# Feed-forward weight sums: two of four made by accumulating transfers instead of VectorE

## The chip, the cores and the metric

The kernel runs on one core of a Trainium2 chip. The metric is the device time of one launch, in microseconds (us). Names of engines: PE is TensorE (PEld its weight loads), DVE is VectorE, ACT is ScalarE, POOL is GpSimd, SP is SyncE; SPq, ACTq and POOLq are the DMA issues of those engines.

## The reference

A block with attention and a mixture of experts is followed by two transformer layers. The change touches the feed-forward part of these two layers alone (256 tokens, width 1024, hidden width 4096, all float32):

```python
for layer in range(DEPTH_2):
    ...
    x = x + mixed @ w_out[layer]
    h = rms_norm_2(x, mlp_norm_w[layer])
    x = x + jnp.square(jax.nn.relu(h @ w_up[layer])) @ w_down[layer]
return rms_norm_2(x, final_norm_w)
```

## The kernel before

**Stages.** First come the conditioning and attention of the first block, then 32 experts (bound by their weight transfers), then the two layers. Every weight is streamed once from HBM, in tiles of 128 x 2048 float32 (1 MB). A layer has 48 tiles: 0 to 11 are input projections, 12 to 15 the output projection `w_out` (its second half is line L1159), 16 and 17 the first four chunks of the up projection by plain matmuls (L629), 18 to 46 the 29 tiles "seven" (14 of the up projection, 15 of the down projection), 47 the last two chunks of the down projection.

**A seven tile.** It is a matrix product of 2 x 2 blocks with seven block products instead of eight (Strassen's scheme in Winograd's form). Four of the products need sums of weight blocks, s1 to s4, and sums of token blocks, t1 to t4. PE's order in `pe_seven` is: `a11` by b11 (no sum), s2, s1, s3, s4, `a12`, `a22`; one product is 8 matmul records (L1223), a tile is 56. The token sums are made once for each set of tokens by `dve_differences` (`diff_ready`).

**Weight sums.** `dve_weight_sums` makes all four on DVE, each by one TENSOR_TENSOR of 128 x 512: s1 = a21 + a22 (L2387), s3 = a11 - a21 (L2389), s2 = s1 - a11 (L2391), s4 = a12 - s2 (L2393); then `sum_ready` goes up. They lie in two buffers used in turn, which PE hands back with `sum_used` after its fifth product. The sums of tile i + 2 stand in DVE's program behind the combination of tile i's products (`dve_seven`, L2416 to L2422). The sums of the layer's tile 0 stand ahead of the norm of the feed-forward input: DVE adds the residual (L2315) and the squares (L2230), makes the sums, then runs the norm (L1772, L1775, L2187) and `dve_differences` (L2400 to L2407), for which PE's first seven tile waits.

**Transfers.** SP issues every weight tile in order. A layer's tiles go round `RL` = 8 ring buffers, so tile t is issued when tile t - 8 is handed back (`slot_free`). A tile is handed back within the first matmuls of the next tile.

**POOL** runs a few transfers for the first block, a fold of 256 columns in each layer (`pool_fold`), and nothing in the feed-forward part.

Of the kernel before, what the change touches and what calls it, by code (L numbers as in the profile page):

```python
# [141 lines left out]
RL = 8  # L142
# [195 lines left out]
def memory(g):  # L338
# [107 lines left out]
    g.sums = [g.ring[RL + n] for n in range(2)]  # L446
    g.cq_turned, g.ck_turned = (g.ring[RL][:, n * 4 * S:(n + 1) * 4 * S].rearrange("p (c t) -> p c t", c=4) for n in range(2))
# [3 lines left out]
    rest = [apart(a, n) for a in (g.ring[RL + 2], g.ring[RL + 3], g.m_all[:, KC * S:2 * KC * S]) for n in range(4)]  # L451
# [89 lines left out]
def sp_program(sp, g):  # L541
# [194 lines left out]
def pe_unread(e, g, n):  # L736

    e.wait_ge(g.s["ones_set"], 1)
    twice = g.c("ones").unsqueeze(1).to_broadcast([P, 2, P])
# [154 lines left out]
def pe_route(e, g):  # L894
    for k in (4, 5, 6):
        pe_logits(e, g, k)
    pe_turn_tokens(e, g, 2, 0)
    pe_logits(e, g, 7)
    u = g.take(e, ("ss", 1), 6)
    e.wait_ge(g.s["sq_added"], ADDED[1])  # L900
    for tt in range(ST):
        ins = e.matmul(u.ap[:, tt:tt + 1], g.sq[:, 0, tt * P:(tt + 1) * P], g.c("ones", 0, 1), start=tt == 0, stop=True, skip_group_check=True)
    g.last(u, ins)
    pe_turn_tokens(e, g, 0, 7)
    pe_turn_tokens(e, g, 1, 1)
# [8 lines left out]
    e.wait_ge(g.s["none_set"], 1)  # L914
# [288 lines left out]
def pe_seven(e, g, l, i):  # L1203
# [5 lines left out]
    (a11, a12), (a21, a22) = quarters(w)  # L1209
    s1, s2, s3, s4 = (g.sums[i % 2][:, n * 512:(n + 1) * 512].rearrange("p (k c) -> p k c", k=4) for n in range(4))  # L1210
# [221 lines left out]
def act_first(e, g, A):  # L1432
# [21 lines left out]
    e.dma_start(g.posi[:, :], g.dram["pos"].to_broadcast([P, S])).then_inc(s["pos_in"], 16)  # L1454
# [107 lines left out]
def act_layer(e, g, l):  # L1562
# [383 lines left out]
def dve_angles(e, g):  # L1946
# [14 lines left out]
    e.wait_ge(s["pos_in"], 16)  # L1961
    e.wait_ge(s["cst_in"], 16)
# [274 lines left out]
def dve_layer(e, g, l):  # L2237
# [100 lines left out]
    for i in range(SEVENS):  # L2338
# [3 lines left out]
        elif b == of - 1:  # L2342
# [3 lines left out]
            two = g.x[:, 2 * mp:2 * mp + 2, :].rearrange("p c t -> p (c t)")  # L2346
            ins = e.tensor_tensor(two, two, g.pair_c, ALU.add)
# [32 lines left out]
def dve_weight_sums(e, g, l, i):  # L2380

    w = g.filled(e, layer_tile(l, 18 + i))
    (a11, a12), (a21, a22) = quarters(w)
    s1, s2, s3, s4 = (g.sums[i % 2][:, n * 512:(n + 1) * 512].rearrange("p (k c) -> p k c", k=4) for n in range(4))
    if i >= 2 or l:
        e.wait_ge(g.s["sum_used"], SEVENS * l + i - 1)
    g.step.up(e.tensor_tensor(s1, a21, a22, ALU.add))  # L2387
    first = g.step.n
    g.step.up(e.tensor_tensor(s3, a11, a21, ALU.subtract))  # L2389
    e.wait_ge(g.step.sem, first)  # L2390
    g.step.up(e.tensor_tensor(s2, s1, a11, ALU.subtract))  # L2391
    g.after(e)
    e.tensor_tensor(s4, a12, s2, ALU.subtract).then_inc(g.s["sum_ready"], 1)  # L2393


def dve_differences(e, g, a, diff, t1=None):
# [6 lines left out]
    g.step.up(e.tensor_tensor(t1, b12, b11, ALU.subtract))  # L2403
# [169 lines left out]
def pool_program(e, g):  # L2573
    s = g.s
    e.memset(g.c("ones"), 1.0).then_inc(s["ones_set"], 1)
# [11 lines left out]
    e.memset(g.none, 0.0).then_inc(s["none_set"], 1)  # L2587
# [115 lines left out]
```

## Time and profile before

| | us |
|---|---|
| median of the runs shown (2) | 1376.43 |
| lowest, highest | 1376.09, 1376.78 |
| span of the profiled execution | 1375.2 |
| PE busy in it | 1336.9 |
| DVE busy in it | 634.6 |
| ACT busy in it | 299.1 |
| POOL busy in it | 7.8 |

The profile's page states the span, from the first to the last instruction; it gives no other time for that execution. The median of the runs is 1.2 us above the span. Busy times can overlap; a time counts for the end only where nothing else covers it.

### The profile page before, as it was taken

The page shows a single profiled execution, that of the slowest core. Times are in us where ns is not written, and L with a number is a line of the kernel's source. Part 1 is how long each engine was busy: PE and PEld are TensorE (multiplying, and loading weights), DVE is VectorE, ACT ScalarE, POOL GpSimd, SP SyncE. Part 2 cuts the span into 40 slices and gives each one's busy share as a digit, 9 for nine tenths or more (in the row PEclk, how much of TensorE's full clock was granted, in tenths as well). Part 3 has the DMA queues.
Part 4 walks back from the last instruction along what each step waited for, and adds up shares of the span by engine and source line. Part 5 has one row for each costly group of instructions (what it writes and reads, how often), then busy time and mean ns, then how long its engine had stood idle before and what let it go on. Part 6 is the DMA issues. An engine that isn't in the chain of part 4 may idle for free.

```text
span 1375.2 us, 21077 instructions
## 1 busy us (share of the span) xinstructions
PE 1336.9 (97%) x8758; PEld 997.9 (73%) x8758; DVE 634.6 (46%) x1424; ACT 299.1 (22%) x596; POOL 7.8 (1%) x18
## 2 busy tenths in 40 slices
PE   8999999999999998888999999999999999999997
PEld 5888886444334433333588789999998878999996
DVE  2477565111100100010378847774555784777454
ACT  2234102112112112111243521220013352122000
POOL 0000000000000000000000000000000000000000
PEclk9999999999999999999999999999999999999999
DMA  9997785999999999999954144545444414454410
GB/s 393 361 413 263 300 358 186 421 414 421 421 421 421 420 421 421 421 421 420 417 224 154 62 153 154 183 156 183 155 159 151 151 62 154 158 180 158 180 62 32
DMA packets 52096, 364.63 MB, mean 265 GB/s; under 512 B 6160, under 2 KB 6464, under 8 KB 8992
## 3 DMA queue, kind: packets, MB, share of 16 engines
q1 hardware_dynamic: 49392, 355.49, 65.6%
q10 hardware_dynamic: 1888, 5.04, 1.3%
q0 software_dynamic: 720, 2.72, 0.5%
q8 instruction: 72, 1.18, 0.4%
q14 instruction: 24, 0.20, 0.1%
HBM read 359.02 MB, written 2.11 MB: 263 GB/s over the span
## 4 chain that ended last, share of the span: by engine, by line
PE 87%; DMA 11%; DVE 1%; ACT 0%; issue 0%; DVEq 0%; POOL 0%; POOLq 0%
PE bank L1223 26%; PE bank L629 20%; PE bank L944 17%; DMA ring<-in_weights 6%; PE bank L641 5%; DMA ringx<-in_weights 4%; PE bank L955 3%; PE bank L1368 2%; PE bank L1159 2%; PE bank L757 2%; PE bank L929 1%; PE bank L1272 1%; PE bank L1323 1%; PE bank L741 1%; PE bank L701 1%; PE bank L1349 1%
## 5 line engine op out<-in xcount | busy, mean ns | idle before, releaser
L944 PE MATMUL bank<-ring,cst 128*64 128x512 f32 x648 | 196.4, 595 | 7.6 <-DMA ring<-in_weights 6.1
L629 PE MATMUL bank<-h,ring 128*128 128x256 f32 x832 | 184.1, 381 | 0.1
L629 PEld LDWEIGHTS bank<-h,ring 128*128 128x128 f32 x832 | 156.9, 190 | 22.8 <-issue 1.7
L944 PEld LDWEIGHTS bank<-ring,cst 128*64 128x64 f32 x648 | 60.7, 137 | 102.0 <-issue 99.7
L2151 DVE TENSOR_TENSOR act<-act,bank 128x512 f32<-128x512 f32 (+1 forms) x17 | 11.1, 656 | 245.0 <-PE bank L944 245.0
L1223 PE MATMUL bank<-hid,ring 128*128 128x128 f32 x912 | 115.6, 275 | 0.0
L1223 PE MATMUL bank<-h,ring 128*128 128x128 f32 x896 | 113.8, 275 | 0.0
L1223 PEld LDWEIGHTS bank<-hid,ring 128*128 128x128 f32 x912 | 108.6, 192 | 0.0
L944 PE MATMUL bank<-ringx,cst 128*64 128x512 f32 x264 | 101.0, 596 | 6.8 <-DMA ring<-in_weights 4.2
L1223 PEld LDWEIGHTS bank<-h,ring 128*128 128x128 f32 x896 | 107.0, 192 | 0.1
L1223 PE MATMUL bank<-sq,ring 128*128 128x128 f32 x720 | 95.1, 275 | 0.0
L944 PE MATMUL bank<-ring,a_s 128*64 128x512 f32 x312 | 90.5, 597 | 0.8 <-DMA ring<-in_weights 0.7
L1223 PEld LDWEIGHTS bank<-sq,ring 128*128 128x128 f32 x720 | 87.6, 192 | 0.0
L641 PE MATMUL bank<-ring,h 128*128 128x256 f32 x320 | 71.0, 381 | 0.0
L2158 DVE COPY gy<-bank 128x512 f32<-128x512 f32 x16 | 11.1, 692 | 125.4 <-PE bank L944 125.4
L1223 PE MATMUL bank<-ring 128*128 128x128 f32 x512 | 67.6, 275 | 0.0
L641 PEld LDWEIGHTS bank<-ring,h 128*128 128x128 f32 x320 | 60.3, 190 | 9.6 <-issue 1.5
L955 PEld LDWEIGHTS bank<-put,gy 128*128 128x128 f32 x256 | 44.8, 190 | 30.3 <-issue 26.0
L955 PE MATMUL bank<-put,gy 128*128 128x256 f32 x256 | 66.4, 393 | 0.0
L1672 ACT COPY hal<-bank 128x128 f32<-128x128 f32 x36 | 9.5, 265 | 256.3 <-PE bank L1223 256.3
L1223 PEld LDWEIGHTS bank<-ring 128*128 128x128 f32 x512 | 62.3, 192 | 0.0
L944 PEld LDWEIGHTS bank<-ringx,cst 128*64 128x64 f32 x264 | 29.9, 137 | 40.7 <-issue 40.7
(391 smaller groups left out, 1809.5 us busy)
## 6 DMA issues: line engine op xcount, KB each, us to landing
ring<-in_weights SPq DMA_DIRECT2D x261, 1024.0 KB, 10.8
ringx<-in_weights SPq DMA_DIRECT2D x50, 1024.0 KB, 24.5
pool_a<-in_weights SPq DMA_DIRECT2D x10, 1024.0 KB, 20.0
x<-in_weights SPq DMA_DIRECT2D x10, 1024.0 KB, 23.0
ring<-in_weights SPq DMA_DIRECT2D x6, 512.0 KB, 22.8
x<-in_x SPq DMA_DIRECT2D x1, 1024.0 KB, 5.1
pool_a<-in_cst ACTq DMA_DIRECT2D x1, 1024.0 KB, 6.2
bias<-bias_rows POOLq DMA_DIRECT2D x1, 1024.0 KB, 17.2
```

The source lines that it names most:

```text
L629: ins = e.matmul(u.ap[:, 0:S], w[:, k * width + j * P:k * width + (j + 1) * P], acts[:, k, :], start=k == 0, stop=k == kc - 1)
L641: ins = e.matmul(u.ap[:, 0:256], acts[:, k, tt * P:(tt + 1) * P], w[:, k * 256:(k + 1) * 256], start=k == 0, stop=k == KC - 1)
L701: ins = e.matmul(u.ap[32 * q:32 * q + 32, 0:256], g.spread[:, k, :], w[:, k * 256:(k + 1) * 256], start=m == 0, stop=m == 1)
L741: e.matmul(g.bank[5][:, 0:S].rearrange("p (n t) -> p n t", n=2), g.c("ones"), twice, start=True, stop=True)
L757: ins = e.matmul(u.ap[:, 0:S], w[:, k * 256 + jj * P:k * 256 + (jj + 1) * P], g.h[:, k, :], start=k == 0, stop=k == KC - 1)
L929: ins = e.matmul(g.bank[bank + k // 4][:, (k % 4) * P:(k % 4 + 1) * P], g.h_tok[:, tt, k * P:(k + 1) * P], g.pick[:, tt * P:(tt + 1) * P], ...
L944: ins = e.matmul(g.bank[bank][ex * SLOTS:(ex + 1) * SLOTS, :], stat(m, ex), pair[ex][:, m * 512:(m + 1) * 512], start=first and m == 0, st ...
L955: ins = e.matmul(g.bank[4 + oc // 2][:, (oc % 2) * S:(oc % 2 + 1) * S], gy[:, oc * P:(oc + 1) * P], put[:, :], start=p == oc % 2 == 0, sto ...
L1159: ins = e.matmul(out[j].ap[:, jj * S:(jj + 1) * S], w[:, k * 256 + jj * P:k * 256 + (jj + 1) * P], g.mix[:, k, :], start=False, stop=k == ...
L1223: ins = e.matmul(u.ap[:, at * P:(at + 1) * P], a[:, k, :], act[:, k, :], start=k == 0 and (of == 1 or (b == 0 and first)), stop=k == 3 and ...
L1272: ins = e.matmul(us[j].ap[HB * b:HB * b + HB, lv * HB:(lv + 1) * HB], k, q, start=True, stop=True)
L1368: e.matmul(u.ap[:, jj * S:(jj + 1) * S], w[:, k * 256 + jj * P:k * 256 + (jj + 1) * P], g.mix[:, k, :], start=k == jj == 0, stop=False, sk ...
```

## The change

**Order of the columns.** The host lays a seven tile out as a22, a11, a12, a21, 512 columns each, with signs chosen so that only additions are left in the weight sums.

**Transfers.** SP loads the first 1536 columns of a seven tile (a22, a11, a12; 768 KB). A second SP transfer (`sp_pair`) reads a21 and writes it twice into a pair buffer (512 KB written). POOL then issues a transfer with `accum_op=ALU.add` (`pool_add`) that adds a22 and a11 from HBM to the two copies (512 KB): s1 = a21 + a22 and s3 = a21 + a11. There are four pair buffers (`ADDED_AHEAD`). They take the place of ring buffers 7 and 8, so `RL` is 7. The sums s2 and s4, in two buffers as before, move to ring buffer 9.

**Order and waits.** In SP's program the copy for tile t - 3 stands behind the load of tile t; it waits until the pair buffer is free (`sum_used`, four tiles back). POOL's accumulation m waits for its copy (`slot_filled`) and for accumulation m - 2. DVE waits for accumulation m (`pair_added_0` or `_1`) before the two sums that it still makes. POOL's 29 accumulations of a layer stand behind that layer's fold.

**Signs.** DVE makes s2 = s1 + a11 and s4 = a12 + s2. Token sums t2 and t4 become `scalar_tensor_tensor` operations (four operations in `dve_differences`, as before). ACT's ReLU of two chunks becomes two operations of 256 columns, the second with scale -1. The residual update after a down block becomes an add and a subtract of 256 columns in place of one add of 512.

**Elsewhere.** Three semaphores are merged into others (`memory_set`; the positions' transfer now counts on `cst_in`).

```diff
-RL = 8
+RL = 7
+ADDED_AHEAD = 4
@@ memory
-    g.sums = [g.ring[RL + n] for n in range(2)]
+    g.added = [g.ring[RL + n // 2][:, (n % 2) * 1024:(n % 2 + 1) * 1024] for n in range(ADDED_AHEAD)]
+    g.sums = [g.ring[RL + 2][:, n * 1024:(n + 1) * 1024] for n in range(2)]
@@ sp_program
     for t in range(T_LAYERS, N_TILES):
         slot_free(sp, g, t)
-        sp.dma_start(g.ring[SLOT[t]][:, :], w[t]).then_inc(g.slot_filled[SLOT[t]], 16)
+        cols = slice(0, 1536 if seven_number(t) is not None else TILE)
+        sp.dma_start(g.ring[SLOT[t]][:, cols], w[t][:, cols]).then_inc(g.slot_filled[SLOT[t]], 16)
+        m = seven_number(t - ADDED_AHEAD + 1)
+        if m is not None:
+            sp_pair(sp, g, w[t - ADDED_AHEAD + 1], m)
...
+def sp_pair(sp, g, tile, m):
+    if m >= ADDED_AHEAD:
+        sp.wait_ge(g.s["sum_used"], m - ADDED_AHEAD + 1)
+    else:
+        sp.wait_ge(g.s["col_a"], 6 * PAIRS)
+        sp.wait_ge(g.s["col_b"], 6 * PAIRS)
+    b = m % ADDED_AHEAD
+    twice = tile[:, 1536:2048].unsqueeze(1).to_broadcast([P, 2, 512])
+    sp.dma_start(g.added[b].rearrange("p (n c) -> p n c", n=2), twice).then_inc(g.slot_filled[RL + b], 16)
@@ pool_program
     for l in range(DEPTH2):
         pool_fold(e, g, l)
+        for i in range(SEVENS):
+            pool_add(e, g, l, i)
+
+def pool_add(e, g, l, i):
+    m = SEVENS * l + i
+    if m >= 2:
+        pair_added(e, g, m - 2)
+    pair_copied(e, g, m)
+    tile = g.dram["weights"][layer_tile(l, 18 + i)]
+    e.dma_start(g.added[m % ADDED_AHEAD], tile[:, 0:1024], accum_op=ALU.add).then_inc(g.s["pair_added_%d" % (m % 2)], 16)
@@ act_program
-        e.activation(two, two, ACT.Relu).then_inc(s["relu_done"], 1)
+        e.activation(plus, plus, ACT.Relu)
+        e.activation(minus, minus, ACT.Relu, scale=-1.0).then_inc(s["relu_done"], 1)
@@ dve_program, after a down block
-            ins = e.tensor_tensor(two, two, g.pair_c, ALU.add)
+            step.up(e.tensor_tensor(plus, plus, g.pair_c[:, 0:S], ALU.add))
+            ins = e.tensor_tensor(minus, minus, g.pair_c[:, S:2 * S], ALU.subtract)
@@ dve_weight_sums
-    if i >= 2 or l:
-        e.wait_ge(g.s["sum_used"], SEVENS * l + i - 1)
-    g.step.up(e.tensor_tensor(s1, a21, a22, ALU.add))
-    first = g.step.n
-    g.step.up(e.tensor_tensor(s3, a11, a21, ALU.subtract))
-    e.wait_ge(g.step.sem, first)
-    g.step.up(e.tensor_tensor(s2, s1, a11, ALU.subtract))
+    if m >= 2:
+        e.wait_ge(g.s["sum_used"], m - 1)
+    pair_added(e, g, m)
+    g.step.up(e.tensor_tensor(s2, s1, a11, ALU.add))
     g.after(e)
-    e.tensor_tensor(s4, a12, s2, ALU.subtract).then_inc(g.s["sum_ready"], 1)
+    e.tensor_tensor(s4, a12, s2, ALU.add).then_inc(g.s["sum_ready"], 1)
@@ dve_differences
-    g.step.up(e.tensor_tensor(t2, b22, t1, ALU.subtract))
+    g.step.up(e.scalar_tensor_tensor(out=t2, in0=t1, scalar=-1.0, in1=b22, op0=ALU.mult, op1=ALU.subtract))
     g.after(e)
-    e.tensor_tensor(t4, b21, t2, ALU.subtract).then_inc(g.s["diff_ready"], 1)
+    e.scalar_tensor_tensor(out=t4, in0=t2, scalar=-1.0, in1=b21, op0=ALU.mult, op1=ALU.subtract).then_inc(g.s["diff_ready"], 1)
```

SP's queue in the first layer, kernel before: the first row is the load of tile 18, the first seven tile.

```order
L574 DMA ring2<-in_weights 128x2048 [waits slots_freed]
L574 DMA ring3<-in_weights 128x2048 [waits slots_freed]
L574 DMA ring4<-in_weights 128x2048 [waits slots_freed]
L574 DMA ring5<-in_weights 128x2048 [waits slots_freed]
L574 DMA ring6<-in_weights 128x2048 [waits slots_freed]
```

SP's queue in the changed kernel, also from the load of tile 18 on (L602 is the copy of a21).

```order
L578 DMA ring4<-in_weights 128x1536 [waits slots_freed]
L578 DMA ring5<-in_weights 128x1536 [waits slots_freed]
L578 DMA ring6<-in_weights 128x1536 [waits slots_freed]
L578 DMA ring0<-in_weights 128x1536 [waits slots_freed]
L602 DMA ring7<-in_weights 128x2x512 [waits col_b,col_a]
L578 DMA ring1<-in_weights 128x1536 [waits slots_freed]
L602 DMA ring7<-in_weights 128x2x512 [waits col_b,col_a]
L578 DMA ring2<-in_weights 128x1536 [waits slots_freed]
L602 DMA ring8<-in_weights 128x2x512 [waits col_b,col_a]
```

The first copy (for tile 18) stands behind the load of tile 21, and each later copy behind one more load.

DVE's program at the entry to the feed-forward part of the first layer, kernel before: the last squares, the sums of tile 18, the norm.

```order
L2230 TENSOR_TENSOR sq_111<-sq_111 128x512 [waits dve_step,squares] x2
L2387 TENSOR_TENSOR ring<-ring 128x512 [waits slot_filled_2]
L2389 TENSOR_TENSOR ring<-ring 128x512
L2391 TENSOR_TENSOR ring<-ring 128x512 [waits dve_step]
L2393 TENSOR_TENSOR ring<-ring 128x512 [waits dve_step]
L1772 TENSOR_SCALAR scr_113<-bank 128x256 [waits bank_full_1]
L1775 RECIPROCAL scr_113<-scr_113 128x256 [waits bank_free_1]
```

DVE's program in the changed kernel at the same place.

```order
L2275 TENSOR_TENSOR sq_111<-sq_111 128x512 [waits dve_step,squares] x2
L2435 TENSOR_TENSOR ring<-ring 128x512 [waits pair_added_0,slot_filled_4]
L2437 TENSOR_TENSOR ring<-ring 128x512 [waits dve_step]
L1818 TENSOR_SCALAR scr_113<-bank 128x256 [waits bank_full_1]
L1821 RECIPROCAL scr_113<-scr_113 128x256 [waits bank_free_1]
```

Two operations are gone, and the first of the two that stay waits for the accumulating transfer; the norm stays behind them.

## Rows read from the trace of the kernel before

**Rows 1.** The page, part 1: busy time of each engine, share of the span.

```profile
PE 1336.9 (97%) x8758; PEld 997.9 (73%) x8758; DVE 634.6 (46%) x1424; ACT 299.1 (22%) x596; POOL 7.8 (1%) x18
```

**Rows 2.** Waits of PE from 700 to 1376 us (total us, times, longest).

```profile
PE bank L1323 <- issue: 1.8, 2, 0.9
PE bank L1323 <- ACT mixed L1644: 0.5, 1, 0.5
```

**Rows 3.** Windows: length, busy of PE, PEld, DVE, ACT, POOL, PEclk, DMA share, GB/s.

```profile
845.00:1000.00 155.00, 155.00 (x1391) 155.00 (x1390) 99.99 (x190) 22.75 (x48) 0.00 (x0) 1.00 0.48 170
...
560.00:650.00 90.00, 78.87 (x354) 31.92 (x354) 6.80 (x18) 12.87 (x18) 0.00 (x0) 1.00 1.01 421
```

**Rows 4.** DVE's groups by form, 800 to 1376 us (busy us, mean ns, idle before).

```profile
L2393 DVE TENSOR_TENSOR ring<-ring 128x512 f32<-128x512 f32 x58 | 40.1, 692 | 2.0
L2387 DVE TENSOR_TENSOR ring<-ring 128x512 f32<-128x512 f32 x58 | 39.8, 686 | 37.6 <-PE bank L1223 37.6
...
L2433 DVE SCALAR_TENSOR_TENSOR hm<-bank,cst 128x512 f32<-128x512 f32 x8 | 5.5, 686 | 3.2 <-PE bank L1323 3.2
```

**Rows 5.** Timeline, entry to the first layer's feed-forward part (start us, us).

```profile
821.31 0.68 DVE L2387 TENSOR_TENSOR ring<-ring 128x512 f32<-128x512 f32 x1
...
823.84 0.41 DVE L1772 TENSOR_SCALAR scr<-bank 128x256 f32<-128x256 f32 x1
...
831.51 0.69 DVE L2407 TENSOR_TENSOR sq<-h,sq 128x512 f32<-128x512 f32 x1
...
832.92 1.07 PEld L1223 LDWEIGHTS bank<-h,ring 128*128 128x128 f32 x8
833.13 1.05 PE L1223 MATMUL bank<-h,ring 128*128 128x128 f32 x8
```

**Rows 6.** Timeline, the same entry in the second layer.

```profile
1164.65 0.69 DVE L2387 TENSOR_TENSOR ring<-ring 128x512 f32<-128x512 f32 x1
...
1174.86 0.69 DVE L2407 TENSOR_TENSOR sq<-h,sq 128x512 f32<-128x512 f32 x1
...
1176.48 1.05 PE L1223 MATMUL bank<-h,ring 128*128 128x128 f32 x8
```

**Rows 7.** Timeline of SP's issues: hand-backs of tile 14, 15 and 17, then layer two's 14.

```profile
815.63 0.33 SPq L574 DMA_DIRECT2D ring<-in_weights  x1
...
819.08 0.33 SPq L574 DMA_DIRECT2D ring<-in_weights  x1
...
833.55 0.33 SPq L574 DMA_DIRECT2D ring<-in_weights  x1
...
1158.97 0.33 SPq L574 DMA_DIRECT2D ring<-in_weights  x1
```

**Rows 8.** SP's 11 loads of 1 MB from 800 to 860 us, issue to landing.

```profile
DMA to landing us min/median/max: 4.6/4.8/6.5
```

**Rows 9.** DMA issues of POOL: xcount, KB each, median us to landing.

```profile
bias<-bias_rows POOLq DMA_DIRECT2D x1, 1024.0 KB, 17.2
cst<-in_cst POOLq DMA_DIRECT2D x1, 640.0 KB, 10.2
...
pool_a<-in_cst POOLq DMA_DIRECT2D x1, 320.0 KB, 6.7
```

**Rows 10.** Timeline of the fourth seven tile: start of that tile, its s2 product, DVE's sums for it.

```profile
846.90 0.68 DVE L2387 TENSOR_TENSOR ring<-ring 128x512 f32<-128x512 f32 x1
...
851.89 1.06 PE L1223 MATMUL bank<-h,ring 128*128 128x128 f32 x8
...
852.78 1.06 PE L1223 MATMUL bank<-sq,ring 128*128 128x128 f32 x8
```

**Rows 11.** Windows at the end of the span, columns as in rows 3.

```profile
1366.00:1367.00 1.00, 0.56 (x2) 0.15 (x2) 0.40 (x2) 0.00 (x0) 0.00 (x0) 1.00 0.08 16
...
1368.50:1369.00 0.50, 0.00 (x0) 0.00 (x0) 0.50 (x2) 0.08 (x1) 0.00 (x0) 0.66 0.00 0
1369.00:1370.00 1.00, 0.00 (x0) 0.00 (x0) 1.00 (x2) 0.23 (x1) 0.00 (x0) 0.50 0.00 0
```

More of the change, by code:

```diff
@@ L186 @@
 SLOT, USE, BEFORE = slots()
-SEMS = ("x_in prm_in prm_late ones_set none_set cst_in late_in tab_in pos_in pool_in row_out bias_in mask_in slots_in result_out slots_freed ada_freed "
+PAIR_USES = [sum(SLOT[t] == RL + b for t in range(T_LAYERS)) for b in range(ADDED_AHEAD)]
+SEMS = ("x_in prm_in prm_late memory_set pair_added_0 pair_added_1 cst_in late_in tab_in pool_in row_out bias_in mask_in slots_in result_out slots_freed ada_freed "
         "cact_ready cact_spread ada_rows ada_turned ada_placed select_ready squares sq_added recip root h_scaled h_shifted trig_ready rope_ready lb_diff lb_exp "
@@ L450, in memory @@
     g.h_diff = [apart(near_cols, n) for n in range(3)]
-    rest = [apart(a, n) for a in (g.ring[RL + 2], g.ring[RL + 3], g.m_all[:, KC * S:2 * KC * S]) for n in range(4)]
+    rest = [apart(a, n) for a in (g.ring[RL + 3], g.ring[RL + 4], g.m_all[:, KC * S:2 * KC * S]) for n in range(4)]
     g.hid_diff = [rest[3 * b:3 * b + 3] for b in range(4)]
@@ L573, in sp_program, with seven_number @@
         slot_free(sp, g, t)
-        sp.dma_start(g.ring[SLOT[t]][:, :], w[t]).then_inc(g.slot_filled[SLOT[t]], 16)
+        cols = slice(0, 1536 if seven_number(t) is not None else TILE)
[3 more added lines that the diff above has]
+            sp_pair(sp, g, w[t - ADDED_AHEAD + 1], m)
+    for t in range(N_TILES - ADDED_AHEAD + 1, N_TILES):
+        if seven_number(t) is not None:
+            sp_pair(sp, g, w[t], seven_number(t))
+def seven_number(t):
+    l, j = divmod(t - T_LAYERS, T_LAYER)
+    return SEVENS * l + j - 18 if t >= T_LAYERS and 18 <= j < 18 + SEVENS else None
+def sp_pair(sp, g, tile, m):
[7 more added lines that the diff above has]
+    sp.dma_start(g.added[b].rearrange("p (n c) -> p n c", n=2), twice).then_inc(g.slot_filled[RL + b], 16)
 SQUARES = {0: 0, 1: 4, 2: 12, 3: 28, 4: 32, 5: 40, 6: 44}
@@ L1183, in quarters, with sums_of, pair_copied, pair_added @@
 def quarters(w):
-    v = w[:, :].rearrange("p (j k i c) -> p j k i c", j=2, k=4, i=2)
-    return [[v[:, j, :, i, :] for j in range(2)] for i in range(2)]
+    return [w[:, n * 512:(n + 1) * 512].rearrange("p (k c) -> p k c", k=4) for n in range(3)]
+def sums_of(g, m):
+    a, b = g.added[m % ADDED_AHEAD], g.sums[m % 2]
+    return [s[:, n * 512:(n + 1) * 512].rearrange("p (k c) -> p k c", k=4) for n in range(2) for s in (a, b)]
+def pair_copied(e, g, m):
+    b, use = m % ADDED_AHEAD, m // ADDED_AHEAD
+    e.wait_ge(g.slot_filled[RL + b], 16 * (PAIR_USES[b] + use + 1))
+def pair_added(e, g, m):
+    e.wait_ge(g.s["pair_added_%d" % (m % 2)], 16 * (m // 2 + 1))
 def token_quarters(a):
@@ L1208, in pe_seven @@
     w = g.filled(e, layer_tile(l, 18 + i))
-    (a11, a12), (a21, a22) = quarters(w)
-    s1, s2, s3, s4 = (g.sums[i % 2][:, n * 512:(n + 1) * 512].rearrange("p (k c) -> p k c", k=4) for n in range(4))
+    a22, a11, a12 = quarters(w)
+    s1, s2, s3, s4 = sums_of(g, SEVENS * l + i)
     (b11, t1), (b21, b22) = token_quarters(g.h if i < UPS else g.hid[:, 8 * b:8 * b + 8, :])
@@ L2574, in pool_program @@
     s = g.s
-    e.memset(g.c("ones"), 1.0).then_inc(s["ones_set"], 1)
+    e.memset(g.c("ones"), 1.0).then_inc(s["memory_set"], 1)
     g.evac(e, "row")
@@ L2666 @@
     assert weights.shape[0] == N_TILES, weights.shape
+    for l in range(DEPTH2):
+        sevens = weights[layer_tile(l, 18):layer_tile(l, 18 + SEVENS)]
+        v = sevens.reshape(SEVENS, P, 2, 4, 2, 128)
+        sevens[:] = np.concatenate([v[:, :, j, :, i].reshape(SEVENS, P, 512) for i, j in ((1, 1), (0, 0), (0, 1), (1, 0))], 2)
     prm = np.zeros((P, N_PRM), np.float32)
```

25 lines of the change are left out of this document (13 added, 12 removed).

## The prediction

> **What bounds the kernel now.** I read the page first: PE is busy for 97% of the span, DVE for 46%, POOL for 1% [rows 1]. A busy share is no proof, because matmul ends are modelled, so I read PE's waits next: from 700 us to the end PE waits 2.3 us in all, and none of it is in the seven tiles [rows 2]. Then the windows: from 845 to 1000 us, inside the seven tiles, PE and its weight loads are busy for all 155 us at granted clock 1.00, that is 2.4 GHz, while DVE is busy for 100 us and the DMA engines for 0.48 of the time [rows 3]. The reader should see that the feed-forward part is bound by PE alone. A tile of 1.05 MB at 170 GB/s comes to 6.2 us, and the 56 matmul records of a tile at 155 / 1391 us each to 6.24 us. The change takes nothing from PE. Where it takes work from DVE inside that stretch, it takes it from an engine with slack. It can gain only where DVE's own chain is what PE waits for, and lose wherever a new transfer comes late.
>
> One such place exists in each layer, the entry to the seven tiles. In the first layer DVE starts the sums of tile 18 at 821.31, starts the norm at 823.84 and ends the last token sum at 832.20 (831.51 + 0.69); PE's weight load for the first seven product starts at 832.92 [rows 5]. PE comes there straight from the up chunks, so DVE's chain is 0.7 us from being late. In the second layer the same chain ends at 1175.55 and PE starts at 1176.48, with the weight load some 0.1 us ahead: 0.8 us of slack [rows 6]. PE's own waits name no other place where the DVE operations that change stand near its path [rows 2].
>
> **The change part by part.**
>
> DVE's sums, steady state. Two of four operations go, 58 times in all. The first to start is at 821.31 and the norm behind the fourth at 823.84, so four take 2.53 us; two dependent ones take about 1.3 us (a start-to-start of 0.7 with the wait, 0.6 without), so 1.2 us is saved for each tile. Inside the tiles this lies beside PE and is worth 0. At the entry it is worth at most 1.2 us to DVE's chain.
>
> The token sums. `scalar_tensor_tensor` on 512 columns takes 686 ns where the trace has it, and `tensor_tensor` 684 to 692 ns [rows 4]: 0. This row reads PSUM and not SBUF, but the sizes agree, so I take it.
>
> ACT's ReLU in two halves and the residual in two halves add an operation each. ACT is busy for 22.75 of 155 us and DVE is relieved by more than it is charged [rows 3]: 0. The cover is PE's 6.2 us for a tile; if it were gone, each would cost some 0.2 us.
>
> The ring of seven instead of eight. In the tiles a load lands 4.8 us after its issue [rows 8], and it is issued seven tiles ahead instead of eight, some 40 us ahead of use: 0. Even the half tiles of the output projection are handed back 3.45 us apart [rows 7], so in the projections it is still over 20 us ahead: 0. The merged semaphores: 0.
>
> The copies and accumulations, steady state. Take the fourth seven tile. The load that stands ahead of its copy is issued at 833.55, just after PE starts the first seven tile [rows 7], so the copy goes out at 833.88. A lone 1 MB load lands after 4.8 us, of which 1.05 MB at the full 421 GB/s are 2.5 us and 2.3 us are fixed [rows 3, 8]. The load of 0.79 MB and the copy of 0.52 MB move in 3.1 us, so the copy lands at about 833.55 + 2.3 + 3.1 = 839.0. Before, DVE reached these sums at 846.90 and PE needs the result at 852.78 [rows 10]; with 1.3 us for the two operations and 0.1 us to pass on, the accumulation must land by 851.4. It has 12.4 us. Two accumulations may be in flight, which asks for the same: under 12.5 us each. Transfers that POOL issued took 6.7 us for 320 KB, 10.2 us for 640 KB and 17.2 us for 1 MB, all beside a full load queue [rows 9]. For 512 KB this gives about 8.8 us when the engines are full and, from SP's lone load (4.8 less 1.25 us), 3.5 us when they are idle. Both are under 12.4: I take 0 for tiles 19 to 46. POOL waits only for its own chain there, and nothing else stands in its queue but the second layer's fold, which comes much later.
>
> DMA load. In this stretch 1.05 MB for each tile cost a share of 0.48. The new traffic is 1.31 MB of plain writes, 0.60 by that price, and 0.52 MB accumulated, 0.24 if it costs what a copy costs and 0.48 if the destination must be read as well: 0.84 to 1.08. By the price of the full queue (421 GB/s at share 1.01) it is 0.70 to 0.90. No row shows an accumulating transfer, so its cost is open between these, and upward. I take the lower half, because the engines work more densely when queues are full [rows 3]: PE stays the bound.
>
> The Trainium skill, DMA: Bandwidth & Descriptors, section "Issuing engines are not separate DMA queues", says that transfers of SP and GpSimd run on the same 16 DMA engines and interleave. By that rule the 58 accumulations buy no bandwidth of their own, and a late one is queued among SP's loads. Its page Collectives: The Full Stack, section "The bandwidth ceiling: the fold count and why AG ≠ RS ≠ AR", says that a reducing transfer is slower because it needs two source reads. By that rule the upper of each pair of shares above would hold; no row here can show it.
>
> The first pair of each layer. This is the term that counts. The copy for tile 18 stands behind the load of tile 21, which now waits for tile 14 to be handed back, at 815.63 [rows 7]. Copy and load land at 815.63 + 2.3 + 3.1 = 821.0. Only then can POOL issue. The accumulation lands between 3.5 us (SP's idle case) and 10.2 us (POOL's 640 KB) later. The engines are occupied with tile 22 and the second copy, issued from 819.08 on, for some 3.1 us after 821, so I take 6.2 us, a little over the middle of 3.5 and 8.8: it lands at 827.2. DVE was ready for it at 821.31 and now starts at 827.3, 6.0 us later. It gets back 1.2 us, so norm and token sums end 4.8 us later; the slack takes 0.7 us, and PE stands still for 4.1 us. What is queued behind DVE's wait is the whole norm, for which PE's 29 tiles wait. In the second layer the hand-back of tile 14 is at 1158.97 and DVE's sums at 1164.65 [rows 6, 7], the same 5.68 us apart: 4.0 us of stall. Together 8.1 us. The bounds: 3.5 us gives 1.4 us for each layer, 2.8 in all; 10.2 us gives 8.1 for each, 16 in all. Nothing brings this below zero, because the copy alone lands when DVE is ready, and the accumulation comes on top.
>
> PE's clock after the stall. At the end of the span the last matmuls lie in 1366 to 1367; the granted clock is 0.66 in 1368.50 to 1369.00 and 0.50, that is 1.2 GHz, from 1369 on [rows 11]. So about 2 us without a matmul were enough there, and a stall of 4 us may let the clock fall. No row shows how long PE then works at half clock. The bounds are 0 and one tile's time, 6.2 us, for each layer; I take 1.5 us, nearer to zero, because PE resumes at once with dense work. That is 3.0 us in all.
>
> Sum: 8.1 + 3.0 = 11.1 us on the profiled execution's 1375.2. That execution's span lies 1.2 us under the median of the runs, and I carry this difference over: 1376.4 + 11.1 = 1387.5 us.
>
> **The rivals.**
>
> *No stall, no change.* The accumulation lands within some 2 us of its copy, or PE's up chunks end later than I read. For it: a slack of 0.7 us and 1.2 us of relief for DVE, so 1.9 us of lateness is free. Against it: even SP's lone loads need 4.6 us [rows 8]. Time 1376.4. Should the accumulations not do what they say, for instance land far earlier than any transfer here, this is the case too.
>
> *The DMA engines become the bound.* Mechanism: an accumulation takes over 12.5 us, since two in flight must serve a tile every 6.24 us. It decides when the destination read, or the adding itself, makes the share exceed 1. At 1.08 the excess is 0.5 us a tile, 27 us over 54 tiles; if an accumulation took the 17.2 us of POOL's 1 MB transfer [rows 9] a tile would take 8.6 us, 2.4 us more, 127 us in all. With the entry stalls: 1415 to 1515, say 1500. For it: no row prices the adding. Against it: a share of 0.70 to 0.90 by the price of the full queue.
>
> *Faster.* DVE's relief shortens something on PE's path. For it: the entry is tied to DVE's chain. Against it: with 0.7 us of slack there, and no wait of PE in the tiles [rows 2], there is nothing to win; two later ends in a layer change nothing. It could be worth 1 us at most: 1375.
>
> *Later pairs are late too.* Copies 2 to 4 of a layer share the engines with the first, and some of tiles 19 to 21 wait a few us: 1395 to 1408.
>
> **How the numbers follow.** Late first pair, 1387.5 (its own range 1379 to 1401): 0.62. No change: 0.11. DMA bound: 0.16. Later pairs late too: 0.09. Faster: 0.02. The range must leave out no more than 0.2; it leaves out the DMA-bound case and a little on either side: 1376.5 to 1408. A measurement of this kernel can tell about 2% from no change, that is 27.5 us, so "slower" begins at 1404: the DMA-bound case and a piece of the fourth, 0.18. Faster by over 2%: 0.01. The rest, 0.81, is within 2%.
>
> **What would show it right or wrong.** Right: DVE idle before its first weight sum of each layer for 5 to 7 us, released by the accumulating transfer; PE idle for about 4 us before the first seven product, twice; a granted clock under 1.00 just after; no wait of PE in tiles 19 to 46; DVE busy some 70 to 75 us less (116 operations fewer by 0.6 us); the DMA share in the tiles between 0.7 and 1. Wrong: a seven tile that takes longer than 6.3 us, a share at 1.0, or a wait for `pair_added` in every tile (the adding is dear); no wait at the entry (the transfer is fast); a stall of PE that comes from the ring of seven.

## The result and the profile after

The changed kernel takes 1425.12 us, the median of 2 runs (1422.25 to 1427.98), beside 1376.43 us before: ratio 1.0352, 95% interval 1.0335 to 1.0368. It is slower by 3.5%, some 48.7 us, above the upper end of the predicted range. The profiled execution has a span of 1425.7 us, 50.5 us longer.

The page of the changed kernel, part 1, answers to [rows 1].

```profile
PE 1351.9 (95%) x8758; PEld 1009.4 (71%) x8758; DVE 567.5 (40%) x1316; ACT 301.7 (21%) x624; POOL 58.1 (4%) x76
```

DVE lost 67.1 us of work. PE makes the same 8758 matmuls, but is busy for 15.0 us longer. With no instruction added, its matmuls went slower: the granted clock was 0.50 behind both entries and behind four of the waits in the tiles. PE's waits from 700 us to the end of the changed kernel (us in total, times, longest) stand beside [rows 2]:

```profile
PE bank L1267 <- DVE ring L2437: 22.6, 13, 4.8
PE bank L1267 <- DVE sq L2451: 11.8, 2, 6.1
PE bank L1367 <- issue: 1.8, 2, 0.9
PE bank L1367 <- ACT mixed L1688: 0.5, 1, 0.5
```

The first two rows are new. L2451 is the last token sum, so its two waits are the two entries. L2437 is s2, DVE's first own weight sum, so those 13 waits lie inside the tiles. The account closes: 11.8 (entries) + 22.6 (tiles) + 15.0 (PE busy for longer) = 49.4 of the 50.5 us.

**The tiles.** Windows of the changed kernel, columns as in [rows 3]: the tiles, then what follows each entry stall, then what follows two waits inside the tiles, of 3.4 and 4.8 us.

```profile
850.00:1000.00 150.00, 142.20 (x1245) 140.99 (x1244) 64.69 (x129) 23.96 (x61) 18.14 (x21) 0.99 0.97 268
...
839.00:843.00 4.00, 4.00 (x19) 4.00 (x20) 3.80 (x10) 0.00 (x0) 0.00 (x0) 0.50 0.89 257
843.00:847.00 4.00, 4.00 (x28) 4.00 (x28) 0.00 (x0) 0.00 (x0) 0.83 (x1) 0.74 0.49 149
...
1207.00:1210.00 3.00, 3.00 (x14) 3.00 (x15) 3.00 (x9) 0.00 (x0) 0.00 (x0) 0.50 0.99 244
...
1263.16:1270.00 6.84, 6.84 (x61) 6.84 (x62) 6.22 (x13) 1.51 (x4) 1.73 (x2) 1.00 0.95 279
...
1375.62:1381.00 5.38, 5.38 (x25) 5.38 (x26) 1.38 (x2) 0.00 (x0) 1.73 (x2) 0.50 0.62 131
```

The DMA share in the tiles rose from 0.48 to 0.97, near the middle of the prediction's 0.84 to 1.08 and above the lower half that it took, while the bytes rose only from 170 to 268 GB/s. The share alone does not say that the engines are the bound: PE is still busy for 142 of 150 us. What does say what binds is the chain of waits of the changed kernel between 899 and 930 us (start, us, what), back from one late product to the one before it:

```profile
899.77 0.70 DVE ring L2435
900.48 0.02 issue
900.50 0.70 DVE ring L2437
901.20 0.04 issue
901.24 5.86 PE bank L1267 x50
907.11 0.02 issue
907.12 0.33 SPq L578
907.45 0.04 issue
907.50 8.66 DMA ring<-in_weights
916.16 0.02 issue
916.18 0.02 POOLq L1225
916.20 0.49 issue
916.69 10.91 DMA ring<-in_weights
927.60 0.03 issue
927.62 0.05 DVEq L1230
927.67 0.04 issue
927.72 0.70 DVE ring L2435
928.42 0.02 issue
928.45 0.70 DVE ring L2437
929.15 0.04 issue
929.19 18.37 PE bank L1267 x162
```

It is a loop. PE works 5.86 us from the late product to the hand-back of its tile. SP then issues a load, and the copy behind it goes out at 907.50 and lands after 8.66 us. POOL (its wait for the copy is L1225) issues the accumulation at 916.69, which lands after 10.91 us. DVE makes s2, and PE's product starts at 929.19, 27.95 us after the one from which the loop began. Four buffers allow four tiles for it, 4 x 6.25 = 25.0 us. All but the two landings come to 27.95 - 8.66 - 10.91 = 8.4 us, so the two landings together may take **16.6 us**. Here they take 19.6.

That this is no exception is seen in the issues of the changed kernel from 850 to 1000 us (xcount, KB each, median us to landing), with the DMA queues above them (q1 is SP's, q0 POOL's: packets, MB, share of the 16 engines):

```profile
q1 hardware_dynamic: 9142, 28.83, 56.0%
q0 software_dynamic: 3059, 11.15, 40.4%
...
ring<-in_weights SPq DMA_DIRECT2D x21, 768.0 KB, 6.8
ring<-in_weights SPq DMA_DIRECT2D x22, 512.0 KB, 8.9
ring<-in_weights POOLq DMA_DIRECT2D x21, 512.0 KB, 8.6
```

Copy and accumulation together take 8.9 + 8.6 = 17.5 us in the median, 0.9 more than the loop has.

**The entry.** Timeline of the changed kernel at the first layer, beside [rows 5]:

```profile
822.62 0.91 POOL L2649 DMA_DIRECT2D ring<-in_weights  x1 [65.81 <-DMA ring<-in_weights]
...
829.14 0.69 DVE L2435 TENSOR_TENSOR ring<-ring 128x512 f32<-128x512 f32 x1 [8.12 <-DMA ring<-in_weights]
...
838.98 2.05 PE L1267 MATMUL bank<-h,ring 128*128 128x128 f32 x8 [6.06 <-DVE sq L2451]
```

The chain of waits of the same stretch has both landings (start, us, what): SP's copy, then POOL's accumulation.

```profile
815.69 6.63 DMA ring<-in_weights
...
822.62 6.42 DMA ring<-in_weights
```

DVE starts 7.8 us later than before (821.31) and PE 5.85 us later (833.13). The eight records of PE's first product take 2.05 us instead of 1.05: the granted clock is 0.50, that is 1.2 GHz. The second layer's entry reads alike, with a wait of 5.76 us.

### The profile page after: what moved, and what is told of

Read it like the earlier page. It is cut to its first block, busy times and chain, and to the rows that moved or that the text cites. A ratio compares the mean times of both kernels' runs of the same rounds, so it can differ in the third digit from the quotient of the medians.

```text
span 1425.7 us, 21174 instructions
## 1 busy us (share of the span) xinstructions
PE 1351.9 (95%) x8758; PEld 1009.4 (71%) x8758; DVE 567.5 (40%) x1316; ACT 301.7 (21%) x624; POOL 58.1 (4%) x76
## 3 DMA queue, kind: packets, MB, share of 16 engines
q0 software_dynamic: 9072, 33.13, 12.2%
## 4 chain that ended last, share of the span: by engine, by line
PE 73%; DMA 22%; DVE 3%; issue 1%; ACT 0%; SPq 0%; DVEq 0%; POOLq 0%
DMA ring<-in_weights 18%; PE bank L657 18%; PE bank L1267 17%; PE bank L972 17%; PE bank L669 5%; DMA ringx<-in_weights 4%; PE bank L983 3%; PE bank L1412 2%; PE bank L785 2%; PE bank L1187 2%; PE bank L957 1%; PE bank L1316 1%; PE bank L1367 1%; PE bank L729 1%; PE bank L1393 1%
## 5 line engine op out<-in xcount | busy, mean ns | idle before, releaser
L1267 PE MATMUL bank<-h,ring 128*128 128x128 f32 x896 | 116.6, 279 | 11.8 <-DVE sq L2451 11.8
L1267 PE MATMUL bank<-hid,ring 128*128 128x128 f32 x912 | 119.0, 280 | 0.0
L2435 DVE TENSOR_TENSOR ring<-ring 128x512 f32<-128x512 f32 x58 | 40.1, 691 | 192.7 <-DMA ring<-in_weights 185.1
L1267 PEld LDWEIGHTS bank<-hid,ring 128*128 128x128 f32 x912 | 112.2, 197 | 0.0
L2196 DVE TENSOR_TENSOR act<-act,bank 128x512 f32<-128x512 f32 (+1 forms) x17 | 11.1, 656 | 245.4 <-PE bank L972 245.4
L1267 PE MATMUL bank<-ring 128*128 128x128 f32 x512 | 72.8, 288 | 13.4 <-DVE ring L2437 13.4
L1267 PEld LDWEIGHTS bank<-ring 128*128 128x128 f32 x512 | 66.5, 203 | 14.8 <-DVE ring L2437 14.8
L2649 POOL DMA_DIRECT2D ring<-in_weights x58 | 50.2, 866 | 478.4 <-DMA ring<-in_weights 478.4
```

What stands on the lines that cost most here:

```text
L1267: ins = e.matmul(u.ap[:, at * P:(at + 1) * P], a[:, k, :], act[:, k, :], start=k == 0 and (of == 1 or (b == 0 and first)), stop=k == 3 and ...
L2435: g.step.up(e.tensor_tensor(s2, s1, a11, ALU.add))
L2649: e.dma_start(g.added[m % ADDED_AHEAD], tile[:, 0:1024], accum_op=ALU.add).then_inc(g.s["pair_added_%d" % (m % 2)], 16)
```

## The experiments

Two theories were set against each other. By the **chain theory** PE waits because the landings of copy and accumulation together take longer than the pair buffers allow. By the **rate theory** the 16 DMA engines can't move a tile's bytes in 6.24 us, and no order or number of buffers helps. In the expectations that speak of theory A and theory B, A is nearest to the rate theory, and B is a chain that is too long whatever the load of the engines. Diffs are against the changed kernel unless they say otherwise; "..." marks lines left out. Each ratio is taken against runs of the kernel before made beside it (medians 1376.76 to 1376.88).

**All additions on DVE.** The new signs, ReLU halves, residual halves and a ring of seven stay; copies and accumulations go, and DVE makes all four sums by additions in the two buffers.

```diff
@@ sp_program
-        cols = slice(0, 1536 if seven_number(t) is not None else TILE)
...
-            sp_pair(sp, g, w[t - ADDED_AHEAD + 1], m)
...
@@ dve_weight_sums
-    pair_added(e, g, m)
...
+    g.step.up(e.tensor_tensor(s1, a21, a22, ALU.add))
+    first = g.step.n
+    g.step.up(e.tensor_tensor(s3, a21, a11, ALU.add))
+    e.wait_ge(g.step.sem, first)
@@ pool_program
...
-            pool_add(e, g, l, i)
```

> No pair buffers, copies or accumulations: tiles are loaded whole in the new column order, and DVE makes all four sums by additions; the ring of seven, the split ReLU and residual and the new token sums stay. Theory: these parts cost nothing, 1375 to 1378 us. Rival, the ring of seven or the longer DVE and ACT operations are part of the loss: 1382 us or more.

Measured 1376.99 us, ratio 1.0001 (0.9992 to 1.0011), DMA share 0.47. All the small edits are worth nothing, as steps of the prediction had it.

**No transfer by POOL.** The copies stay, POOL's accumulations go, and DVE waits for the copy.

```diff
-    pair_added(e, g, m)
+    pair_copied(e, g, m)
@@ pool_program
-        for i in range(SEVENS):
-            pool_add(e, g, l, i)
```

> POOL's accumulations are left out, and DVE waits for the copy of a21 alone (s1 and s3 are just a21). What stays is the loads of 768 KB, the copies of 512 KB, the ring of seven and all signs. Theory A and B alike: the copy lands when DVE is ready (822.5 against 821), DVE's shorter sums cover it, no wait in the tiles: 1376 to 1379 us. Rival, the copies in 2 KB pieces are themselves the burden: a stall in the entries and some waits in the tiles, 1385 us or more.

Measured 1377.13 us, ratio 1.0002 (0.9992 to 1.0011). A copy lands after 6.0 us, a load after 4.2. The share is 0.69 at 216 GB/s, against 0.47 at 169 without the copies (the kernel with all additions on DVE). So the late copy alone costs nothing, even at the entry.

**POOL's transfer without the adding.**

```diff
-    e.dma_start(g.added[m % ADDED_AHEAD], tile[:, 0:1024], accum_op=ALU.add).then_inc(...)
+    e.dma_start(g.added[m % ADDED_AHEAD], tile[:, 0:1024]).then_inc(...)
```

> POOL's 58 transfers of 512 KB stay, with their waits and places, but copy instead of adding (so the sums s1 and s3 are left out of the computation). Theory A, the DMA engines are full because the adding makes each accumulation read its destination too: the accumulations' 2.8 us of engine time a tile fall to about 1.4, the share in the tiles falls from 0.97 to about 0.8, the waits inside the tiles (22.6 us in the changed kernel) vanish, the entry stall shrinks by about 1.3 us a layer: 1388 to 1396 us. Theory B, the chain of copy and accumulation is too long for four buffers whatever the engines' load: landing times stay near 8 us, 1410 to 1422 us. Rival C, the adding costs nothing beside the copy itself: 1425 us.

Measured 1394.81 us, ratio 1.0123 (1.0102 to 1.0144). PE's waits, and the queues and issues from 850 to 1000 us, of this kernel:

```profile
PE bank L1267 <- DVE sq L2451: 10.3, 2, 5.6
PE bank L1267 <- DVE ring L2437: 1.8, 1, 1.8
```

```profile
q1 hardware_dynamic: 9985, 32.10, 67.5%
q0 software_dynamic: 3168, 11.54, 21.5%
...
ring<-in_weights SPq DMA_DIRECT2D x21, 768.0 KB, 5.9
ring<-in_weights SPq DMA_DIRECT2D x24, 512.0 KB, 8.1
ring<-in_weights POOLq DMA_DIRECT2D x23, 512.0 KB, 7.0
```

The time lies in theory A's band, though the share fell to 0.90 only and not to 0.8, and theory B's 1410 and more falls. This run alone doesn't tell too little engine time from landings made long by loaded engines; the runs with three and six buffers do. Three things follow. The entry stall is nearly all there without any adding (10.3 of 11.8 us): it belongs to two transfers in a row. The waits in the tiles are nearly gone (1.8 of 22.6), at landings of 15.1 us together, under 16.6. And the adding doubles what the transfer costs the engines: 0.215 x 150 us for 22.0 transfers of 0.524 MB is 1.47 us each, with adding 0.404 x 150 / 21.3 = 2.85 us. The rule that I had cited from the Trainium skill, page Collectives: The Full Stack, section "The bandwidth ceiling: the fold count and why AG ≠ RS ≠ AR", that a reducing transfer needs two source reads, is stated there for collectives; the ratio of 1.9 in these rows agrees with it. That the destination is what is read here is argued, not shown. The other cited rule (the Trainium skill, page DMA: Bandwidth & Descriptors, section "Issuing engines are not separate DMA queues") agrees too: POOL's plain transfers alone move SP's copies from 6.0 to 8.1 us and its loads from 4.2 to 5.9.

**One sum of four.** Full load of the tile, a copy of 256 KB, an accumulation of 256 KB; DVE makes three sums.

```diff
-        cols = slice(0, 1536 if seven_number(t) is not None else TILE)
+        cols = slice(0, TILE)
...
-    sp.dma_start(g.added[b]..., twice)
+    sp.dma_start(g.added[b][:, 0:512], tile[:, 1536:2048])
...
+    g.step.up(e.tensor_tensor(s3, w[:, 1536:2048]..., a11, ALU.add))
...
-    e.dma_start(g.added[...], tile[:, 0:1024], accum_op=ALU.add)
+    e.dma_start(g.added[...][:, 0:512], tile[:, 0:512], accum_op=ALU.add)
```

> One sum of four by the transfers: tiles are loaded whole, a21 is copied once (256 KB), POOL adds a22 to it (256 KB), DVE makes s3, s2 and s4; order and waits as in the changed kernel. Theory A: the engines' work for a tile is 2.9 us for the load, 0.7 for the copy and 1.4 for the adding, 5.0 us or a share of 0.8, so no waits in the tiles; the entry stays late (the accumulation of 256 KB lands some 5 us after its copy, DVE gets back 0.6 us only): 1386 to 1394 us. Theory B, a chain too long at any load: waits in the tiles, 1400 us or more.

Measured 1389.29 us, ratio 1.009 (1.0073 to 1.0106), in theory A's band, at a share of 0.87. Half the bytes still land after 6.5 + 6.5 = 13.0 us; no wait is left in the tiles, 7.8 us at the entries.

**The first four copies of a layer early**, each right behind the load of its own tile.

```diff
+        m = seven_number(t)
+        if m is not None and m % SEVENS < ADDED_AHEAD:
+            sp_pair(sp, g, w[t], m)
         m = seven_number(t - ADDED_AHEAD + 1)
-        if m is not None:
+        if m is not None and m % SEVENS >= ADDED_AHEAD:
```

> The first four copies of each layer are issued right behind the loads of their own tiles 18 to 21 instead of three loads later; nothing else changes. If the entry stalls (6.1 and 5.8 us) and the half clock behind them (about 3.5 us each) are a loss of their own, both vanish: 1404 to 1409 us. Rival, the DMA engines are the bound in the tiles and only pass the lost time on to later waits: 1416 to 1425 us.

Measured 1405.24 us, ratio 1.0195 (1.0178 to 1.0212). No entry wait is left; 19.7 us of waits in the tiles stay, at landings of 8.8 + 8.7 us. By the medians the entries with their clock were worth 20 us and the tiles the rest; the account of the profiled execution gives the entries 16.0 (11.8 of waits, 4.2 of clock), so some 4 us lie in the spread of the runs or are not accounted for.

**Copies in pieces of 4 KB.** The host stores a21 twice, so that a copy reads rows of 4 KB instead of 2 KB; alone, and with the early copies.

```diff
-    sp.dma_start(g.added[b].rearrange("p (n c) -> p n c", n=2), twice).then_inc(...)
+    sp.dma_start(g.added[b], g.dram["pairs"][m]).then_inc(...)
...
```

> The host stores a21 twice, one copy behind the other, so that SP's copy reads and writes rows of 4 KB instead of 2 KB pieces; bytes, order and waits are those of the changed kernel. In the runs without POOL's transfers the copies raised the engines' time for a tile from 2.9 us (0.47 of 6.25) to 4.3 us (0.69 of 6.25), 1.4 us for a net 0.26 MB. Theory A1, the price is in the short pieces: the engines' work for a tile falls from 6.7 us to about 6.0 us, under PE's 6.25 us, so the waits inside the tiles (22.6 us) vanish and only the entry stalls (11 us) and the half clock behind them (about 3.5 us each) stay: 1391 to 1397 us. Rival A2, the price is in the bytes: 1420 to 1427 us.

> The 4 KB rows of the run before and the early copies together. Theory A with A1: entry stall and waits in the tiles have separate causes, both gone: 1377 to 1381 us, no better than the kernel before, because PE is the bound there. Rival, they share one cause or the load stays over PE's pace: 1390 us or more.

Measured 1412.03 us (1399.38 to 1418.09), ratio 1.0225 (1.0176 to 1.0275), between the two figures expected, and 1391.42 us, ratio 1.011 (1.0085 to 1.0134), where I had expected nearly all of the loss to go. Larger pieces save engine time (SP's queue moved 31.85 MB at a share of 0.559, the changed kernel's 28.83 MB at 0.560) but shorten the landings only to 8.1 + 7.8 and 8.0 + 8.3 us, just under the 16.6, and 16.9 and 8.2 us of waits stay in the tiles. The medians alone don't order these two. Single copies land after 6.7 to 11.9 and 6.2 to 12.2 us; that the late ones count where the median is near the allowance is argued, not shown.

**Three buffers instead of four**, with the early copies (diff against these). It is the sharpest test, because it changes no byte.

```diff
-ADDED_AHEAD = 4
+ADDED_AHEAD = 3
...
-        m = seven_number(t - ADDED_AHEAD + 1)
+        m = seven_number(t - RL + ADDED_AHEAD)
...
```

> As the early copies, but three pair buffers instead of four; the fourth lies idle, the bytes are the same. Chain theory: the lead falls by one tile from 17.5 to some 11.2 us, less than the chain of 14 to 17 us, so that every tile waits; a tile takes (chain + 5.5) / 3 = 6.6 to 7.5 us instead of 6.24: 1410 to 1450, with a wait of PE or DVE in nearly every tile and a DMA share that falls below 0.95 because the pace falls. Rate theory: the number of buffers beyond two does not matter, 1400 to 1410, share as before 0.95 to 0.97.

Measured 1501.60 us (1493.41 to 1507.06), ratio 1.092 (1.0899 to 1.094): the rate theory (1400 to 1410) falls. The loss is even above my own figure. This kernel's chain of waits shows why:

```profile
898.60 7.49 PE bank L1270 x50
906.09 0.02 issue
906.10 0.33 SPq L578
906.43 0.04 issue
906.47 5.97 DMA ring<-in_weights
...
912.98 8.25 DMA ring<-in_weights
...
922.82 7.49 PE bank L1270 x50
```

The loop's other links come to 24.22 - 5.97 - 8.25 = 10.0 us, not the 5.5 that I had put down; PE's own part alone is 7.49, at a lowered clock. With this kernel's median landings, 7.9 + 8.2, a tile should take (16.1 + 10.0) / 3 = 8.7 us. The 124.8 us lost over the 52 tiles behind the early ones give 6.24 + 2.4 = 8.6. The mean share fell to 0.83, and yet the landings stayed at 16 us: they are long even where the engines have room on average.

**The copy ahead of the load** (diff against the early copies). Early copies, and each later copy issued ahead of the load that it had stood behind.

```diff
+        m = seven_number(t - ADDED_AHEAD + 1)
+        if m is not None and m % SEVENS >= ADDED_AHEAD:
+            sp_pair(sp, g, w[t - ADDED_AHEAD + 1], m)
         slot_free(sp, g, t)
...
-        m = seven_number(t - ADDED_AHEAD + 1)
-        if m is not None and m % SEVENS >= ADDED_AHEAD:
-            sp_pair(sp, g, w[t - ADDED_AHEAD + 1], m)
```

> As the early copies (first four of a layer right behind the loads of their own tiles), and every later copy now stands ahead of the load that it stood behind, so that it is not queued behind 768 KB issued a third of a us before; the bytes are the same. Chain theory (PE waits because copy and accumulation together take longer to land than the 17.5 us that four pair buffers leave): the copy lands some 1.5 to 3 us sooner after its buffer is free, chain 14 to 16 us instead of 16 to 18, most of the 19.7 us of waits go: 1378 to 1390. Rival, rate theory (the 16 DMA engines cannot move a tile's bytes in 6.24 us): the order changes nothing, 1400 to 1408 as with the early copies alone.

Measured 1383.28 us, ratio 1.0043 (1.0032 to 1.0055), in the expected band, but not by the way expected. Timeline of this kernel, SP's copy (L605) and load (L581):

```profile
899.96 0.38 SPq L605 DMA_DIRECT2D ring<-in_weights  x1
901.97 0.33 SPq L581 DMA_DIRECT2D ring<-in_weights  x1
```

The copy lands no sooner after its issue (9.3 us). It is issued 2.0 us ahead of the load instead of 0.37 behind it, because `sum_used` comes before the hand-back of the tile. (The 17.5 us of the expectation was my earlier figure for the allowance; the loop's rows give 16.6.) The allowance grows to 19.0 us, the landings to 9.3 + 9.8 = 19.1, and 4.5 us of waits are left, in 8 pieces of up to 1.0.

**Six pair buffers**, a ring of six, each copy behind the load of its own tile; nothing else.

```diff
-RL = 7
-ADDED_AHEAD = 4
+RL = 6
+ADDED_AHEAD = 6
...
-        m = seven_number(t - ADDED_AHEAD + 1)
+        m = seven_number(t)
         if m is not None:
-            sp_pair(sp, g, w[t - ADDED_AHEAD + 1], m)
+            sp_pair(sp, g, w[t], m)
...
```

> A ring of six and six pair buffers, each copy issued right behind the load of its own tile; pieces of 2 KB and the adding as in the changed kernel. The engines' work for a tile stays at 6.7 us against PE's 6.25, 0.45 us too much, 13 us over the 29 tiles of a layer; two more buffers give a lead of 12.5 us more. Theory A, a lack of throughput that a lead can pay for within a layer: share near 1.0, landing times longer than 9 us, waits nearly gone: 1377 to 1388 us. Rival D, the limit of two accumulations in flight decides: waits stay, 1400 us or more. Theory B, latency alone: waits gone, and landing times and share as in the changed kernel.

Measured 1380.30 us, ratio 1.0026 (1.0015 to 1.0038), in theory A's band and with its signs; rival D falls. Its tiles in the windows:

```profile
850.00:1000.00 150.00, 150.00 (x1345) 150.00 (x1345) 68.07 (x137) 22.43 (x57) 19.89 (x23) 1.00 1.02 295
```

With the landings at 11.0 + 9.7 = 20.7 us, longer than in the changed kernel, PE waits for nothing in the tiles, since six buffers allow 6 x 6.25 - 8.4 = 29.1. A shortage of 0.45 us a tile, as theory A has it, would make the landings longer from tile to tile. They don't grow: copies issued from 850 to 900 us land after 11.1 us in the median and those from 950 to 1000 after 10.8, POOL's after 9.6 and 9.2, and PE does a tile every 6.25 us throughout. So no backlog builds up, and the full traffic of a tile fits into 6.25 us, at a share of 1.02. Neither A nor B as I had put them holds: the chain is too long for four buffers at the landings that loaded engines give.

**All of it**: six buffers, pieces of 4 KB, each copy ahead of the load of its own tile.

```diff
...
+        m = seven_number(t)
+        if m is not None:
+            sp_pair(sp, g, w[t], m)
         slot_free(sp, g, t)
...
```

> All measures together: six pair buffers and six ring buffers, the copy from a second HBM array that holds a21 twice (pieces of 4 KB), each copy ahead of the load of its own tile. Chain theory: lead some 30 us against a chain under 20, no wait in the tiles and none or under 1 us at the entry: 1376 to 1379, equal to the kernel before and never faster, because PE then bounds the tiles as it did. Rival (accumulations cost PE something beyond waits, in SBUF or in its clock): 1380 to 1390 with no waits shown.

Measured 1377.29 us, ratio 1.0002 (0.9993 to 1.0012). The waits that the changed kernel had are all gone, and nothing is won: PE's 6.24 us a tile is the bound, as before.

The runs with POOL's transfers in one table; the two without had no such waits. "Allowed" is the number of buffers times 6.25 us, less 8.4, and 2.4 more where the copy stands ahead of the load. "Landings" are the median copy plus the median POOL transfer from 850 to 1000 us. "PE longer" is PE's busy time over 1336.9 us. Waits and busy time are those of the profiled execution, which took 1418.1 us with 4 KB pieces and 1493.4 with three buffers. All in us.

| kernel | median | allowed | landings | waits in the tiles | at the entries | PE longer |
|---|---|---|---|---|---|---|
| three buffers | 1501.6 | 10.4 | 16.1 | 77.2 | 0 | 37.1 |
| the change | 1425.1 | 16.6 | 17.5 | 22.6 | 11.8 | 15.0 |
| 4 KB pieces | 1412.0 | 16.6 | 15.9 | 16.9 | 11.7 | 11.4 |
| early copies | 1405.2 | 16.6 | 17.5 | 19.7 | 0 | 11.2 |
| plain transfer | 1394.8 | 16.6 | 15.1 | 1.8 | 10.3 | 5.7 |
| 4 KB, early | 1391.4 | 16.6 | 16.3 | 8.2 | 0 | 6.7 |
| one sum | 1389.3 | 16.6 | 13.0 | 0 | 7.8 | 4.1 |
| copy first | 1383.3 | 19.0 | 19.1 | 4.5 | 0 | 0.4 |
| six buffers | 1380.3 | 29.1 | 20.7 | 0 | 3.5 | 0.6 |
| all of it | 1377.3 | over 31 | 16.7 | 0 | 0 | 0 |

## Why the prediction was wrong

**Right.** The small edits at nothing (kernel with additions on DVE). PE as the bound of the tiles before. The entry as a place of loss in each layer, by the mechanism named: DVE waits for the accumulation, and the norm stands behind it.

**The step that failed** is the steady state: "I take 0 for tiles 19 to 46". It measured 22.6 us of waits, and 7.7 us of clock behind them; a tile took 6.75 us from 850 to 1000 us (1245 records, 56 each), over the 6.3 that the prediction named as a sign of being wrong. The lead that it worked out was right: 12.4 us for the accumulation after a copy of 5.1 is 17.5, and less POOL's half us to issue some 17, beside the 16.6 of the loop. What it set against it was wrong. The copy was given 2.3 us fixed and its own and the load's bytes at 421 GB/s, as if the engines were otherwise idle, and so 5.1 us; it measured 8.9. The accumulation, "about 8.8 us when the engines are full", measured 8.6. The low figure for the first was taken together with the high figure for the second, and 5.1 + 8.8 stayed under the lead where 8.9 + 8.6 did not. The same prediction put the share at 0.84 to 1.08 and took "the lower half"; at 0.97 every landing is long, the copy's as well. The two landings should have been taken from one state of the engines. Besides, one early tile stood for all: in the tile that the prediction worked, the fourth, the copy did land after 5.4 us and the accumulation after 5.7, and PE didn't wait; the copy of the fifth took 7.4 us, that of the seventh 10.3.

**Terms that were mis-sized.** The entry stall: 8.1 us expected, 11.8 measured. In the first layer the copy landed at 822.3 and not at 821.0, POOL's transfer began 0.3 us later, and it took 6.4 us where 6.2 was taken. The clock: 3.0 us expected, 15.0 more of PE's busy time measured, some 12 of it by the clock. At the entries it cost 2.8 and 1.4 us (19 records in 4 us and 28 in the next 4, where 36 fit, and 14 in 3 where 27 fit), so 1.5 for each was near (and the 3.5 for each in the expectation of the early copies was not). The clock fell to 0.50 behind four waits in the tiles too, those that end at 971.16, 1025.71, 1305.26 and 1375.62: in the 17.1 us from there to 975.0, 1029.5, 1309.3 and 1381.0 there are 84 records where 153 fit, 7.7 us. What makes up the last 3 us or so was not taken apart.

**The rivals.** The time lies inside what the DMA-bound rival gave, 1415 to 1515, and still that rival is not what happened. It was to decide at an accumulation above 12.5 us; they land after 5.3 to 11.1. It was to be a throughput above 1; six buffers run the same bytes at PE's pace. "Later pairs are late too" was nearest in kind, but it named only tiles 19 to 21 and the start of a layer, where the lateness comes back in every round of the buffers.

**Open.** Why a 512 KB copy at a share of 0.83 (three buffers) still takes 7.9 us, when 6.0 is enough at 0.69, was not taken apart; copies, loads and accumulations are issued in bursts, and how their packets interleave isn't seen in these views. A version with more than two accumulations in flight wasn't tried. The limit of two doesn't show, though: in the chain rows POOL is released by the copy (L1225) and not by the accumulation before last, each of the 58 accumulations starts within 0.9 us of its copy's landing, and six buffers under the same limit leave no wait in the tiles. Why a wait of 1.9 us was followed by a granted clock of 0.50 and one of 3.4 us by 1.00 stays open.

## What to carry to other kernels

When a step is handed from an engine to transfers, add up the whole loop of its buffer: hand-back, issue, every landing in the chain, the engine's own operations. Compare that with buffers times the time of a tile, and take all landings from the same, loaded, state of the engines. An engine with slack is no reason to relieve it: here 67 us of DVE's work were taken away, nearly all of it under PE, and in the best version nothing came back. If a chain of transfers is late by a little in every round, more buffers or an earlier issue can be worth more than fewer bytes: from four buffers with a copy behind the load to six, which also puts the first copies early, the loss went from 48.7 us to some 3.5; half the bytes at four buffers left some 12.

## What the runs showed of the hardware

- A transfer that adds costs the DMA engines 2.85 us of all 16 for 512 KB, the same transfer without adding 1.47; its landing is lengthened far less, 8.6 against 7.0 us. POOL's issue takes 0.86 us in place of 0.53.
- Half the bytes did not halve the landing: 256 KB land after 6.5 us (share 0.87) where 512 KB take 8.6 to 8.9 (share 0.97).
- A busy share near 1 did not mean that PE had to wait: 1.02 went with PE busy for 150 of 150 us. Landings rose with it, but not by it alone: a 512 KB copy took 6.0 us at 0.69, 7.9 at 0.83, 8.9 at 0.97 and 11.0 at 1.02, and in the last version 7.4 at 0.99, in 4 KB pieces.
- Waits cost more than themselves. PE's busy time grew by 15.0 us on 34.4 us of waits in the changed kernel and by 37.1 on 77.2 with three buffers, in good part since the granted clock fell to 0.50 behind the stalls of 6.1 and 5.8 us and behind waits of 4.8, 2.8, 2.4 and 1.9 us. It didn't behind every longer one: after a wait of 3.4 us it stayed at 1.00. Behind eight waits of 1 us or less (copy first) it stayed at 1.00, and PE was busy for 0.4 us longer.
